# Projection stage of a hybrid attention block: x loaded four pieces ahead, reciprocal roots as logarithm and exponential, rotary key late, w_uq in four parts

## Chip, cores and metric

The kernel runs on the eight NeuronCores of one Trainium2 chip. The metric is device time in microseconds of the slowest core. Each core has TensorE (matmuls), VectorE, ScalarE, GpSimd and the SP queue engine; SP, ScalarE and GpSimd also issue DMAs. The cores do not exchange data or wait for one another inside the program.

## The reference

One layer over a sequence of 16 meta tokens and 4096 frames, batch 4, model width 4096. Only what the projection stage computes matters here:

```
u = rmsnorm(h) * norm_pre
z = u @ w_in        # diff q, k, v, gate; latent c_q (1536), c_kv (512); rotary key (64); mla gate
cq  = rmsnorm(cq) * g_cq;    q  = cq @ w_uq      # 16 heads x (128 + 64 rotary)
ckv = rmsnorm(ckv) * g_ckv;  kv = ckv @ w_ukv    # 16 heads x (128 key + 128 value)
k_rope = rope(kr);  q_rope = rope(q_rope)
```

Two attention groups follow (differential attention with ALiBi, and latent attention), each gated with silu; then one output projection with a norm and the residual. rmsnorm needs the reciprocal root of a mean of squares plus 1e-6.

## The kernel before, in words

Two cores share a batch element: each computes keys and values of all 4112 tokens and queries, gates and outputs of its own 2048 tokens. The work is in three stages: A, the projections (`stage_a`), B, the attention, and C, the output projection. The change touches A only.

The instruction order is written out by hand: `P.add` appends an operation to one engine's list, with tokens (`T`) for what it reads and writes; at the end waits on semaphores are derived from them. Each engine works through its own list in order, so an instruction that waits holds up all behind it on that engine. A DMA operation of several transfers (`dma=5`) has one wait ahead of the first and one semaphore for all. Background work is written as generators: `tick()` takes one step of `bg[0]`, and the matmul loops call it at fixed places, so that the background's instructions lie between those of the foreground.

Stage A goes through x in two phases, of four tiles with 512 tokens each, phase 0 also with a tile of 16 meta tokens (t = 4). The weights come in slabs of 256 columns (`load_upto`, on GpSimd's queue, f32 to bf16, three buffers, so slab i+3 waits for the last use of slab i).

- `prep(0, t)` loads a tile of x in 32 pieces of 128x512 f32 on ScalarE's queue into six buffers. For each piece ScalarE makes the scaled bf16 copy (L460), then the square (L466, L468), and VectorE adds the square to a sum (L469). Matmuls are L525 (columns of weights as the stationary operand) and L585 (tokens stationary). `stats` sums over partitions with a matmul (L474) and takes the reciprocal root (`rsqrt`, L426 to L428: VectorE, ScalarE, VectorE); `rtok_of` (L435) turns it to one value a token.
- The first three slabs are done tile by tile while x is read. The first tile's `prep` is written out before any matmul, that of the next tile lies in the ticks (42 a tile). `stats(0, t)` is written out whole after the first block of tile t; the steps of `prep_meta` (L492 to L496) lie in the first block of tile 3.
- Then `lam_of` computes the lambda of the differential attention from four loads, and slabs 3 to 18 of phase 0 run over the resident tiles while `prep(1, t)` reads the other half of x as background on SP's queue, with three buffers, writing it to DRAM (`UT`); phase 1 reads it back. Slab 3 is the rotary key (`job_kr`): after its matmuls VectorE multiplies with sine and cosine tables (L561 to L575), which SP loads behind the matmuls.
- Phase 1 repeats all key and value slabs and adds c_q, queries and gates. Results are evacuated through four bf16 buffers (`stb`) and stored by SP.
- Then the latent part: nine tiles of c_kv (512 tokens, the fifth has 16), each with 16 key blocks (`kn`, matmuls L792, evacuated by VectorE, L795) and 16 value blocks (`vm`, L803, ScalarE L806), 32 stores on SP; `norm_tile` for the next tile lies in the ticks (squares L729, sum L726, scaling L734). It is followed by four tiles of queries with `w_uq` (L825, L838). w_uq (four loads, one token) and the first two loads of c_q (1,536 KB each, SP) are issued ahead of the first c_kv tile.

What the program adds on each queue around the change:

```
for t in range(5):
    if t < 4:
        early[0] = stats(0, t)
        ...
    for i in range(3):
        run_slab(i, t)
```

Of the kernel before, what the change touches and what calls it, by code (L numbers as in the profile page):

```python
# [6 lines left out]
F32 = mybir.dt.float32  # L7
# [256 lines left out]
def build_nc():  # L264
# [50 lines left out]
    with stack:  # L315
# [23 lines left out]
        lams = A.alloc([8], F32)  # L339
        Tc = T("consts")  # L340
# [3 lines left out]
        ci = [0]  # L344

        def cload(dst, src):
            ci[0] += 1
            P.add('sp', lambda e: e.dma_start(out=dst, in_=src), writes=[Tc], dma=1, key=f'c{ci[0]}')

        cload(identf, ident_d)  # L350
        cload(gpre, gpre_d)
        cload(gcq, gcq_d)
        cload(gckv, gckv_d)
        cload(gsubB, gsub_d.partition_broadcast(128))
        P.add('dve', lambda e: e.tensor_copy(out=identb, in_=identf), reads=[Tc], writes=[Tc])
        P.add('dve', lambda e: e.memset(onesb, 1.0), writes=[Tc])
        P.add('dve', lambda e: e.memset(onesf, 1.0), writes=[Tc])
        P.add('dve', lambda e: e.tensor_scalar_mul(out=gsubB, in0=gsubB, scalar1=0.8), reads=[Tc], writes=[Tc])
# [4 lines left out]
            CK=CK, CQ=CQ, UT=UT, RP=RP, onesb=onesb, onesf=onesf, identf=identf, gpre=gpre, gcq=gcq, gckv=gckv, gsubB=gsubB, Tc=Tc,  # L363
# [13 lines left out]
def stage_a(nc, P, A, bank, Tb, DT, c):  # L377
# [3 lines left out]
    onesb, onesf, identf, gpre, gcq, gckv, gsubB, Tc = (c[k] for k in ['onesb', 'onesf', 'identf', 'gpre', 'gcq', 'gckv', 'gsubB', 'Tc'])  # L381
# [24 lines left out]
    def lam_of():  # L406
# [5 lines left out]
        for i in range(4):  # L412
            P.add('sp', lambda e, i=i: e.dma_start(out=lt4[:, i, :], in_=c['lam4_d'][i:i + 1, :].partition_broadcast(128)), writes=[Tlt], dma=1, key=f'lam{i}')
# [73 lines left out]

    def prep_meta():
        xa, Txa = fp.next()
        x3 = xa.rearrange("p (k t) -> p k t", k=32)  # L490
        P.add('sp', lambda e: e.dma_start(out=x3, in_=xTm), writes=[Txa], dma=1, key=('x', id(Txa)))
        P.add('dve', lambda e: e.tensor_tensor(out=uTm, in0=x3, in1=gpre.unsqueeze(2).to_broadcast([128, 32, 16]), op=ALU.mult), reads=[Txa, Tc], writes=[TuTm])  # L492
        P.add('act', lambda e: e.activation(out=xa, in_=xa, func=AF.Square), reads=[Txa], writes=[Txa])
        yield
        P.add('dve', lambda e: e.reduce_sum(out=Rpre[:, 2048:2064], in_=xa.rearrange("p (k t) -> p t k", k=32), axis=AX.X), reads=[Txa], writes=[TRp[4]])
        P.add('pe', lambda e: e.matmul(bank[SSB][:, 0:16], lhsT=onesf, rhs=Rpre[:, 2048:2064], start=True, stop=True), reads=[TRp[4], Tc], writes=[Tb[SSB]])  # L496
        rsqrt(Rpre[:, 2048:2064], bank[SSB][:, 0:16], 1.0 / D, [Tb[SSB]], TRp[4])
        yield
# [38 lines left out]
    def job_fm(dst_fn):  # L537
        def run(t, buf, Tw):
            ti = tile_of(t)
            wv = buf.rearrange("p (k n) -> p k n", k=32)  # L540
            for blk in range(2):
                b = mm_fm(ti, wv, Tw, 128 * blk)
                if early[0] is not None:
                    for _ in early[0]:
                        pass
                    early[0] = None
                dst, dTs = dst_fn(blk, ti)
                evac_scaled(b, ti, dst, dTs)
                tick()
        return run  # L550

    def job_kr(t, buf, Tw):
# [103 lines left out]
    for _ in gen:  # L656
        pass
# [761 lines left out]
```

How the kernel before makes its waits and increments, by code:

```python
                def body(eng, ops=ops):  # L143
                    waited = {}
                    for op in ops:
                        w = {}
                        for d in need[id(op)]:
                            k = d.sem.num
                            if k not in w or w[k][1] < d.val:
                                w[k] = (d.sem, d.val)
                        for k, (s, v) in w.items():
                            if waited.get(k, 0) < v:
                                eng.wait_ge(s, v)
                                waited[k] = v
                        if op.fn is None:
                            continue
                        ins = op.fn(eng)
                        if op.dma:
                            if not isinstance(ins, (list, tuple)):
                                ins = [ins]
                            assert len(ins) == op.dma, (op.name, len(ins), op.dma)
                            for i in ins:
                                i.then_inc(op.sem, 16)
                        elif op.sig:
                            assert ins is not None, op.name
                            ins.then_inc(op.sem, 1)
```

## Time and profile before

| | us |
|---|---|
| median of 3 runs | 8583.3 (7669.49 to 8768.4) |
| profiled execution, its own time | 7663.14 |
| its span, slowest core (5) | 7661.6 |
| spans of the eight cores | 7628.7 to 7661.6, granted clock 0.969 to 0.971 |
| TensorE busy | 7024.5 (92%) |
| ScalarE busy | 2313.8 (30%) |
| VectorE busy | 1646.0 (21%) |

The profile is of one execution on its slowest core. PE is TensorE's matmuls, PEld its weight loads, DVE is VectorE, ACT ScalarE, POOL GpSimd, SP the queue engine; ACTq, SPq and POOLq are the issuing sides. "Granted clock" is TensorE's clock as a share of full speed. L123 is a line of the kernel before. Matmuls are pipelined, and a few of their records are missing. A wait is put down to what came last.

### The profile page before, as it was taken

To read this page: it belongs to the slowest core of one execution; us is meant where nothing else is said; L and a number is where in the kernel's file an instruction comes from. 1 tells how busy PE (TensorE), PEld (TensorE's weight loads), DVE (VectorE), ACT (ScalarE), POOL (GpSimd) and SP (SyncE) were. 2 spreads that over 40 slices of the span, in tenths; PEclk is the share of its full clock that TensorE was granted. 3 is DMA by queue.
4 is the path that set the end of the run, shared out by engine and by line. 5 is a ranking of instruction groups with operands and counts; after the bars stand their busy time and mean duration, and the time that the engine had idled before them with its cause. 6 is when DMAs were issued, how large, how long until landed. Compare 5 with 4: busy or idle time off the path is not lost.

```text
span 7661.6 us, 142140 instructions; the slowest of 8 cores (7628.7 to 7661.6 us)
## 1 busy us (share of the span) xinstructions
PE 7024.5 (92%) x55192; PEld 5012.4 (65%) x55192; DVE 1646.0 (21%) x3213; ACT 2313.8 (30%) x4442; POOL 314.3 (4%) x570
## 2 busy tenths in 40 slices
PE   3579999999999999999997999999999999979877
PEld 1234588644688444588885344677778888868767
DVE  2324400011000101111001565233331111132233
ACT  3401111000011000011111324888887877311111
POOL 0000000000000000000000000000011010000000
PEclk9789999999999999999998999999999999989989
DMA  5346732533232222333336432122155565365564
GB/s 119 103 94 153 167 80 51 140 75 63 53 62 55 57 59 54 65 72 82 72 77 138 137 116 84 53 84 91 57 152 152 157 179 148 137 220 187 186 213 175
DMA packets 493084, 846.03 MB, mean 110 GB/s; under 512 B 115140, under 2 KB 354820, under 8 KB 472328
## 3 DMA queue, kind: packets, MB, share of 16 engines
q0 software_dynamic: 73952, 447.75, 24.5%
q1 hardware_dynamic: 380456, 319.96, 14.0%
q10 hardware_dynamic: 38016, 69.22, 3.1%
q8 instruction: 450, 7.37, 0.4%
q14 instruction: 210, 1.72, 0.1%
HBM read 790.93 MB, written 234.12 MB: 134 GB/s over the span
## 4 chain that ended last, share of the span: by engine, by line
PE 80%; DVE 6%; DMA 4%; ACT 4%; issue 3%; SPq 1%; another core or an unknown queue 1%; ACTq 1%; DVEq 0%
PE ps L585 24%; PE ps L525 22%; PE ps L1269 10%; PE ps L985 10%; PE ps L1020 9%; PE ps L825 2%; DMA arena<-xo 1%; PE ps L803 1%; ACT arena L460 1%; PE ps L838 1%; DVE arena L469 1%; ACT arena L468 1%; PE ps L792 1%; ACT arena L1009 1%; DVE arena L1093 1%
## 5 line engine op out<-in xcount | busy, mean ns | idle before, releaser
L525 PE MATMUL ps<-arena 128*128 128x512 bf16 (+1 forms) x9632 | 1997.8, 368 | 172.0 <-ACT arena L460 133.7
L585 PE MATMUL ps<-arena 128*128 128x256 bf16 (+1 forms) x16640 | 1819.3, 273 | 0.0
L585 PEld LDWEIGHTS ps<-arena 128*128 128x128 bf16 (+1 forms) x16640 | 1625.1, 98 | 194.0 <-issue 3.2
L525 PEld LDWEIGHTS ps<-arena 128*128 128x128 bf16 x9632 | 900.2, 98 | 1266.5 <-issue 233.6
L1020 PE MATMUL ps<-arena 128*128 128x129 bf16 (+3 forms) x9216 | 1194.8, 248 | 72.7 <-ACT arena L1009 43.5
L985 PE MATMUL ps<-arena 128*128 128x256 bf16 (+2 forms) x8576 | 1222.7, 261 | 3.2 <-issue 3.2
L1269 PE MATMUL ps<-arena 128*128 128x256 bf16 x8192 | 918.2, 276 | 136.6 <-DMA arena<-MIX 87.8
L1269 PEld LDWEIGHTS ps<-arena 128*128 128x128 bf16 x8192 | 811.0, 99 | 243.4 <-issue 139.7
L1020 PEld LDWEIGHTS ps<-arena 128*128 128x128 bf16 (+1 forms) x9216 | 749.6, 98 | 274.5 <-issue 198.6
L1009 ACT ACTIVATE arena<-ps,arena 128x512 bf16<-128x512 f32 (+3 forms) x1352 | 787.9, 622 | 111.1 <-PE ps L985 56.7
L985 PEld LDWEIGHTS ps<-arena 128*128 128x128 bf16 (+1 forms) x8576 | 713.3, 97 | 117.4 <-issue 45.4
L1006 ACT ACTIVATE arena<-ps 128x512 bf16<-128x512 f32 (+2 forms) x1216 | 687.5, 574 | 177.7 <-PE ps L985 83.0
L534 DVE TENSOR_TENSOR arena<-ps,arena 128x512 bf16<-128x512 f32 (+1 forms) x292 | 190.1, 654 | 2047.5 <-PE ps L525 2035.1
L590 ACT ACTIVATE arena<-ps,arena 128x256 bf16<-128x256 f32 (+1 forms) x264 | 124.8, 474 | 1352.3 <-PE ps L585 1334.4
L1275 ACT ACTIVATE arena<-arena 128x256 bf16<-128x256 f32 x256 | 106.6, 417 | 922.7 <-DVE arena L1272 672.8
L596 ACT ACTIVATE arena<-ps,arena 128x256 f32<-128x256 f32 x256 | 121.4, 474 | 763.2 <-PE ps L585 759.9
L639 POOL DMA_DIRECT2D arena<-w_in x264 | 140.4, 551 | 3391.9 <-PE ps L525 1724.5
L1272 DVE COPY arena<-ps 128x256 f32<-128x256 f32 x256 | 108.0, 424 | 729.9 <-PE ps L1269 715.6
L468 ACT ACTIVATE arena<-arena 128x512 f32<-128x512 f32 x248 | 156.1, 629 | 341.4 <-DVE arena L463 330.0
L469 DVE TENSOR_TENSOR arena<-arena 128x512 f32<-128x512 f32 x248 | 171.6, 692 | 359.7 <-ACT arena L468 359.5
L596 ACT ACT_TABLE_LOAD x2 | 2.6, 1283 | 777.5 <-PE ps L585 777.5
L803 PE MATMUL ps<-arena 128*128 128x512 bf16 (+1 forms) x528 | 138.0, 384 | 67.7 <-DVE arena L795 67.7
(98 smaller groups left out, 2535.0 us busy)
## 6 DMA issues: line engine op xcount, KB each, us to landing
arena<-w_in POOLq DMA_DIRECT2D x264, 512.0 KB, 12.8
arena<-WOB POOLq DMA_DIRECT2D x64, 2048.0 KB, 9.0
arena<-xT ACTq DMA_DIRECT2D x128, 256.0 KB, 2.8
arena<-xT SPq DMA_DIRECT2D x128, 256.0 KB, 3.6
arena<-w_out POOLq DMA_DIRECT2D x16, 2048.0 KB, 33.6
WOB<-arena POOLq DMA_DIRECT2D x16, 2048.0 KB, 10.7
arena<-xo ACTq DMA_DIRECT2D x128, 256.0 KB, 9.6
out<-arena SPq DMA_DIRECT2D x128, 256.0 KB, 5.4
```

Of the source, the lines that this page charges most:

```text
L468: P.add('act', lambda e, xa=xa: e.activation(out=xa, in_=xa, func=AF.Square), reads=[Txa], writes=[Txa])
L469: P.add('dve', lambda e, xa=xa: e.tensor_tensor(out=sm, in0=sm, in1=xa, op=ALU.add), reads=[Txa, Tsm], writes=[Tsm])
L525: P.add('pe', lambda e, k=k: e.matmul(bank[b][:, 0:n], lhsT=wv[:, k, col:col + 128], rhs=ti['u'](k), start=(k == 0), stop=(k == 31)), read ...
L534: P.add('dve', lambda e: e.tensor_tensor(out=sb[:, 0:n], in0=bank[b][:, 0:n], in1=ti['R'], op=ALU.mult), reads=[Tb[b], ti['TR']], writes=[ ...
L585: P.add('pe', lambda e, k=k, c0=c0, nt=nt, b=b: e.matmul(bank[b][0:nt, 0:256], lhsT=ti['u'](k)[:, c0:c0 + nt], rhs=wv[:, k, :], start=(k = ...
L803: P.add('pe', lambda e, k=k: e.matmul(bank[b][0:nt, :], lhsT=cn[:, k, c0:c0 + nt], rhs=wkv[:, k, 2048 + 512 * g:2048 + 512 * g + 512], sta ...
L825: P.add('pe', lambda e, b=b, h=h, k=k, cn=cn: e.matmul(bank[b], lhsT=wq[:, k, 128 * h:128 * h + 128], rhs=cn[:, k, :], start=(k == 0), sto ...
L985: P.add('pe', lambda e, lh=lh, rh=rh, a=a, b_=b_, m=m, i=i, n=len(steps): e.matmul(S[0:nk, 256 * m + a:256 * m + b_], lhsT=lh, rhs=rh, sta ...
L1006: P.add('act', lambda e, o_=o_, i_=i_: e.activation(out=o_, in_=i_, func=AF.Exp, scale=scale), reads=[Tb[sbk]], writes=[Tpt])
L1009: P.add('act', lambda e, o_=o_, i_=i_, ci_=ci_: e.activation(out=o_, in_=i_, func=AF.Exp, bias=abias[0:nk, ci_:ci_ + 1], scale=scale), rea ...
L1020: P.add('pe', lambda e, m=m, qb=qb, rhs=rhs, last=last: e.matmul(bank[OB[2 * qb + m]][:, 0:E + 1], lhsT=pt[0:nk, 256 * m + 128 * qb:256 * ...
L1269: P.add('pe', lambda e, k=k: e.matmul(bank[b][:, 0:256], lhsT=m[:, k, :], rhs=w[:, k, :], start=(k == 0), stop=(k == 31)), reads=[Tw, Tm[0 ...
```

## The change

Everything lies in stage A and in the constants ahead of it. (1) The five constants are loaded by one operation of five transfers, gpre first, where each was an operation that waited for the one before; lambda's four loads likewise. (2) `prep` of phase 0 keeps four loads ahead instead of five, in the same six buffers. (3) `rsqrt` is a logarithm and an exponential on ScalarE. (4) `stats` is taken in single steps, one after the first block of each slab; the meta tokens are loaded at the start and their matmul comes later. (5) The rotary key slab moves from position 3 to 15 in both phases, its tables are loaded one tile ahead, and background work is finished before it. (6) w_uq is loaded as four operations at different times, each with a token of its own, and the first two c_q loads move into the c_kv loop. (7) In `norm_tile` the scaling operations are spread over more ticks.

```diff
+        P.add('sp', lambda e: [e.dma_start(out=dst, in_=src) for dst, src in ((gpre, gpre_d), (identf, ident_d), (gcq, gcq_d), (gckv, gckv_d), (gsubB, gsub_d.partition_broadcast(128)))],
+              writes=[Tc], dma=5, key='c')
...
+        P.add('dve', lambda e: e.memset(epsc, EPS), writes=[Tc])
...
-        for i in range(4):
-            P.add('sp', lambda e, i=i: e.dma_start(out=lt4[:, i, :], in_=c['lam4_d'][i:i + 1, :].partition_broadcast(128)), writes=[Tlt], dma=1, key=f'lam{i}')
+        P.add('sp', lambda e: [e.dma_start(out=lt4[:, i, :], in_=c['lam4_d'][i:i + 1, :].partition_broadcast(128)) for i in range(4)], writes=[Tlt], dma=4, key='lam')
...
     def rsqrt(dst, src, inv, rT, wT):
-        P.add('dve', lambda e: e.tensor_scalar(out=dst, in0=src, scalar1=inv, scalar2=EPS, op0=ALU.mult, op1=ALU.add), reads=rT, writes=[wT])
-        P.add('act', lambda e: e.activation(out=dst, in_=dst, func=AF.Sqrt), reads=[wT], writes=[wT])
-        P.add('dve', lambda e: e.reciprocal(out=dst, in_=dst), reads=[wT], writes=[wT])
+        P.add('act', lambda e: e.activation(out=dst, in_=src, func=AF.Ln, bias=epsc[:, 0:1], scale=inv), reads=rT + [Tc], writes=[wT])
+        P.add('act', lambda e: e.activation(out=dst, in_=dst, func=AF.Exp, scale=-0.5), reads=[wT], writes=[wT])
...
@@ def stats
         P.add('pe', lambda e: e.matmul(bank[SSB], lhsT=onesf, rhs=row, start=True, stop=True), reads=[Trow, Tc], writes=[Tb[SSB]])
-        yield
         rsqrt(row, bank[SSB], 1.0 / D, [Tb[SSB]], Trow)
...
+    def load_meta():
+        P.add('sp', lambda e: e.dma_start(out=acc, in_=xTm), writes=[Tacc], dma=1, key='xm')
+
     def prep_meta():
-        xa, Txa = fp.next()
...
+        P.add('dve', lambda e: e.reduce_sum(out=Rpre[:, 2048:2064], in_=acc.rearrange("p (k t) -> p t k", k=32), axis=AX.X), reads=[Tacc], writes=[TRp[4]])
+        for _ in range(6):
+            yield
         P.add('pe', lambda e: e.matmul(bank[SSB][:, 0:16], lhsT=onesf, rhs=Rpre[:, 2048:2064], start=True, stop=True), reads=[TRp[4], Tc], writes=[Tb[SSB]])
         rsqrt(Rpre[:, 2048:2064], bank[SSB][:, 0:16], 1.0 / D, [Tb[SSB]], TRp[4])
-        yield
+        for _ in range(6):
+            yield
...
@@ def job_fm
-                if early[0] is not None:
-                    for _ in early[0]:
-                        pass
-                    early[0] = None
+                if early[0] is not None and blk == 0:
+                    next(early[0], None)
...
@@ def job_kr
-        ck, Tck = fp.next()
-        sk, Tsk = fp.next()
...
+        if not krt:
+            kr_tables(ti)
+        ck, Tck, sk, Tsk = krt.pop(0)
+        if t < (4 if phase_[0] == 0 else 3):
+            kr_tables(tile_of(t + 1))
...
-        out.insert(3, ('kr', 0, job_kr))
         for sl in range(8):
             out.append(('w', C_DV + 256 * sl, job_tm('v', sl)))
+        out.insert(15, ('kr', 0, job_kr))
...
     load_upto(1)
-    gen = prep(0, 0, xfp, 5, 'act')
-    for _ in gen:
+    load_meta()
+    for _ in prep(0, 0, xfp, 4, 'act'):
         pass
...
-            if t < 3:
-                bg[0] = prep(0, t + 1, xfp, 5, 'act')
-            else:
-                bg[0] = prep_meta()
+            bg[0] = prep(0, t + 1, xfp, 4, 'act') if t < 3 else prep_meta()
         for i in range(3):
             run_slab(i, t)
-        while bg[0] is not None:
-            tick()
+        for gen in (early, bg):
+            while gen[0] is not None:
+                if next(gen[0], 'end') == 'end':
+                    gen[0] = None
...
         load_upto(i + 3)
+        if every[i][0] == 'kr':
+            while bg[0] is not None:
+                tick()
+            fp.items = xfp
...
@@ def norm_tile
         rsqrt(acc[:, 0:n], bank[SSB][:, 0:n], inv, [Tb[SSB]], Tacc)
         yield
+        yield
...
-            if k % 2 == 1:
+            if KC_ == 4 or k % 2 == 1:
                 yield
...
+    def load_wq(rT):
+        j = len(Twq) // 3
+        lo = 16384 + 9216 * j
+        t = heir(*[x for a in range(lo // 16384, (lo + 9215) // 16384 + 1) for x in TuT[a]])
+        Twq.extend([t] * 3)
+        P.add('pool', lambda e: e.dma_start(out=wq[:, 3 * j:3 * j + 3, :], in_=w_uq[:, 9216 * j:9216 * j + 9216].rearrange("p (k n) -> p k n", k=3)), reads=rT, writes=[t], dma=1, key=('wq', j))
...
+        elif t == 1:
+            load_wq([])
...
-    q_load(0)
-    q_load(1)
...
-    Twq = heir(*(TuT[1] + TuT[2] + TuT[3]))
-    P.add('pool', lambda e: [e.dma_start(out=wq[:, 3 * k:3 * k + 3, :], in_=w_uq[:, 9216 * k:9216 * k + 9216].rearrange("p (k n) -> p k n", k=3)) for k in range(4)], writes=[Twq], dma=4, key='wq')
...
     for j, (g0, n) in enumerate(kvt):
...
+        if j in (0, 2, 5):
+            load_wq([Tcn])
+        if j in (1, 4):
+            q_load(j // 4)
```

## Rows read from the trace of the kernel before

**Rows 1.** Busy us by stretch: its length, engines, granted clock, DMA share, GB/s.

```profile
0.00:451.50 451.50, 215.60 (x1004) 91.73 (x1004) 121.24 (x174) 174.81 (x263) 8.22 (x19) 0.84 0.38 97
...
451.50:642.60 191.10, 144.43 (x685) 63.33 (x684) 72.38 (x129) 23.64 (x37) 7.48 (x15) 0.88 0.63 140
...
642.60:4119.90 3477.30, 3477.26 (x24675) 2384.05 (x24676) 361.67 (x612) 313.86 (x626) 128.10 (x241) 1.00 0.37 79
...
4119.90:4449.00 329.10, 246.67 (x1151) 107.64 (x1150) 148.92 (x206) 105.27 (x186) 2.12 (x4) 0.90 0.54 147
```

**Rows 2.** Waits of TensorE to 451.5 us: line, awaited, us in total, times, longest.

```profile
PE ps L525 <- ACT arena L460: 133.7, 54, 33.8
...
PE ps L435 <- DVE arena L428: 67.1, 4, 20.9
...
PE ps L496 <- DVE arena L495: 32.3, 1, 32.3
```

**Rows 3.** DMA issues of the first 35 us: transfer, count, size, median us to landing.

```profile
arena<-gpre SPq DMA_DIRECT2D x1, 16.0 KB, 11.9
...
arena<-w_in POOLq DMA_DIRECT2D x4, 512.0 KB, 15.0
```

**Rows 4.** Timeline of the pass over x: start us, us, instruction, idle time before it.

```profile
31.51 1.28 ACT L460 ACT_TABLE_LOAD   x1 [31.51 <-DVE arena L358]
...
54.08 0.72 ACT L460 ACTIVATE arena<-arena 128x512 bf16<-128x512 f32 x1 [1.36 <-DVE arena L469]
...
56.84 0.72 ACT L460 ACTIVATE arena<-arena 128x512 bf16<-128x512 f32 x1 [1.31 <-DVE arena L469]
...
116.58 0.71 ACT L460 ACTIVATE arena<-arena 128x512 bf16<-128x512 f32 x1
...
117.92 0.71 ACT L460 ACTIVATE arena<-arena 128x512 bf16<-128x512 f32 x1
...
118.95 3.58 ACTq L451 DMA_DIRECT2D arena<-xT  x6
...
122.63 0.72 ACT L460 ACTIVATE arena<-arena 128x512 bf16<-128x512 f32 x1 [3.29 <-DMA arena<-xT]
```

**Rows 5.** Timeline around the end of the first tile loop.

```profile
385.35 0.71 ACT L460 ACTIVATE arena<-arena 128x512 bf16<-128x512 f32 x1
...
410.34 41.19 PE L525 MATMUL ps<-arena 128*128 128x512 bf16 x352
...
454.00 32.02 SPq L413 DMA_DIRECT2D arena<-lam  x4
```

**Rows 6.** Waits of TensorE between 451 and 643 us.

```profile
PE ps L525 <- DVE arena L573: 22.7, 4, 8.5
...
PE ps L525 <- DMA arena<-w_kr: 7.6, 1, 7.6
```

**Rows 7.** Waits of TensorE between 4119.9 and 4449 us.

```profile
PE ps L803 <- DVE arena L795: 67.7, 11, 52.2
...
PE ps L792 <- DVE arena L795: 6.1, 2, 3.1
```

**Rows 8.** Timeline of the first latent tile.

```profile
4129.93 3.35 DVE L428 RECIPROCAL arena<-arena 128x512 f32<-128x512 f32 x1 [2.79 <-ACT arena L427]
...
4136.89 49.12 SPq L423 DMA_DIRECT2D KN<-arena  x1
```

**Rows 9.** DMA issues between 4119 and 4195 us.

```profile
arena<-CQ SPq DMA_DIRECT2D x2, 1536.0 KB, 67.8
```

**Rows 10.** DMA issues of x, between 70 and 130 us, then between 145 and 385.

```profile
arena<-xT ACTq DMA_DIRECT2D x22, 256.0 KB, 4.5
...
arena<-xT ACTq DMA_DIRECT2D x84, 256.0 KB, 2.8
```

**Rows 11.** The chain of waits: start us, us, what.

```profile
95.78 18.04 DMA arena<-xT
```

**Rows 12.** ScalarE's groups, whole span: count, busy us, mean ns, idle before.

```profile
L1009 ACT ACT_TABLE_LOAD x1 | 1.3, 1283 | 2.3 <-PE ps L985 2.3
```

More of the change, by code:

```diff
@@ L339, in build_nc @@
         lams = A.alloc([8], F32)
+        epsc = A.alloc([1], F32)
         Tc = T("consts")
@@ L342, in build_nc @@
         const_base = A.off
[L344 to L354, printed above, removed]
+        P.add('sp', lambda e: [e.dma_start(out=dst, in_=src) for dst, src in ((gpre, gpre_d), (identf, ident_d), (gcq, gcq_d), (gckv, gckv_d), (gsubB, gsub_d.partition_broadcast(128)))],
+              writes=[Tc], dma=5, key='c')
         P.add('dve', lambda e: e.tensor_copy(out=identb, in_=identf), reads=[Tc], writes=[Tc])
@@ L362, in build_nc @@
             xT=xT, xTm=xTm, w_in=w_in, w_kr=w_kr, w_uq=w_uq, w_ukv=w_ukv, KD=KD, VD=VD, GD=GD, QD=QD, QN=QN, QR=QR, KN=KN, KR=KR, VM=VM, GM=GM,
-            CK=CK, CQ=CQ, UT=UT, RP=RP, onesb=onesb, onesf=onesf, identf=identf, gpre=gpre, gcq=gcq, gckv=gckv, gsubB=gsubB, Tc=Tc,
+            CK=CK, CQ=CQ, UT=UT, RP=RP, epsc=epsc, onesb=onesb, onesf=onesf, identf=identf, gpre=gpre, gcq=gcq, gckv=gckv, gsubB=gsubB, Tc=Tc,
             lams=lams, Tlam=Tlam, lam4_d=lam4_d, cosk_d=cosk_d, sink_d=sink_d, cosq_d=cosq_d, sinq_d=sinq_d))
@@ L380, in stage_a @@
     CK, CQ, UT, RP = c['CK'], c['CQ'], c['UT'], c['RP']
-    onesb, onesf, identf, gpre, gcq, gckv, gsubB, Tc = (c[k] for k in ['onesb', 'onesf', 'identf', 'gpre', 'gcq', 'gckv', 'gsubB', 'Tc'])
+    epsc, onesb, onesf, identf, gpre, gcq, gckv, gsubB, Tc = (c[k] for k in ['epsc', 'onesb', 'onesf', 'identf', 'gpre', 'gcq', 'gckv', 'gsubB', 'Tc'])
     uo = A.off
@@ L486, in idle @@
             yield
+    def load_meta():
+        P.add('sp', lambda e: e.dma_start(out=acc, in_=xTm), writes=[Tacc], dma=1, key='xm')
     def prep_meta():
-        xa, Txa = fp.next()
[L490 to L493, printed above, removed]
-        yield
-        P.add('dve', lambda e: e.reduce_sum(out=Rpre[:, 2048:2064], in_=xa.rearrange("p (k t) -> p t k", k=32), axis=AX.X), reads=[Txa], writes=[TRp[4]])
+        x3 = acc.rearrange("p (k t) -> p k t", k=32)
+        P.add('dve', lambda e: e.tensor_tensor(out=uTm, in0=x3, in1=gpre.unsqueeze(2).to_broadcast([128, 32, 16]), op=ALU.mult), reads=[Tacc, Tc], writes=[TuTm])
+        P.add('act', lambda e: e.activation(out=acc, in_=acc, func=AF.Square), reads=[Tacc], writes=[Tacc])
+        P.add('dve', lambda e: e.reduce_sum(out=Rpre[:, 2048:2064], in_=acc.rearrange("p (k t) -> p t k", k=32), axis=AX.X), reads=[Tacc], writes=[TRp[4]])
+        for _ in range(6):
+            yield
         P.add('pe', lambda e: e.matmul(bank[SSB][:, 0:16], lhsT=onesf, rhs=Rpre[:, 2048:2064], start=True, stop=True), reads=[TRp[4], Tc], writes=[Tb[SSB]])
         rsqrt(Rpre[:, 2048:2064], bank[SSB][:, 0:16], 1.0 / D, [Tb[SSB]], TRp[4])
-        yield
+        for _ in range(6):
+            yield
         rtok_of(0, 4, 1, 16, Rpre[:, 2048:2064], TRp[4])
@@ L550, in job_fm, with kr_tables @@
         return run
+    krt = []
+    def kr_tables(ti):
+        n, g0 = ti['n'], ti['g0']
+        ck, Tck = fp.next()
+        sk, Tsk = fp.next()
+        P.add('sp', lambda e: e.dma_start(out=ck[:, 0:n], in_=c['cosk_d'][:, g0:g0 + n]), writes=[Tck], dma=1, key=('x', id(Tck)))
+        P.add('sp', lambda e: e.dma_start(out=sk[:, 0:n], in_=c['sink_d'][:, g0:g0 + n]), writes=[Tsk], dma=1, key=('x', id(Tsk)))
+        krt.append((ck, Tck, sk, Tsk))
     def job_kr(t, buf, Tw):
@@ L556, in job_kr @@
         b = mm_fm(ti, wv, Tw, 0)
-        ck, Tck = fp.next()
-        sk, Tsk = fp.next()
-        P.add('sp', lambda e: e.dma_start(out=ck[:, 0:n], in_=c['cosk_d'][:, g0:g0 + n]), writes=[Tck], dma=1, key=('x', id(Tck)))
-        P.add('sp', lambda e: e.dma_start(out=sk[:, 0:n], in_=c['sink_d'][:, g0:g0 + n]), writes=[Tsk], dma=1, key=('x', id(Tsk)))
+        if not krt:
[3 more added lines that the diff above has]
+            kr_tables(tile_of(t + 1))
         P.add('dve', lambda e: e.tensor_tensor(out=ck[:, 0:n], in0=ck[:, 0:n], in1=ti['R'], op=ALU.mult), reads=[Tck, ti['TR']], writes=[Tck])
@@ L752, in stage_a @@
     wkv, Twkv = uT[:, 0].rearrange("p k t -> p (k t)").rearrange("p (k n) -> p k n", k=4), heir()
+    uflat = uT.rearrange("p a k t -> p (a k t)")
+    wq = uflat[:, 16384:16384 + 36864].rearrange("p (k n) -> p k n", k=12)
+    Twq = []
+    def load_wq(rT):
[4 more added lines that the diff above has]
+        P.add('pool', lambda e: e.dma_start(out=wq[:, 3 * j:3 * j + 3, :], in_=w_uq[:, 9216 * j:9216 * j + 9216].rearrange("p (k n) -> p k n", k=3)), reads=rT, writes=[t], dma=1, key=('wq', j))
     for t in range(4):
@@ L844, in stage_a @@
     A.note(uo, 32768, Twkv)
-    A.note(uo + 32768, 73728, Twq)
+    A.note(uo + 32768, 73728, *Twq)
     for i in range(2):
```

6 lines of the change are left out of this document (2 added, 4 removed).

## The prediction

> **What bounds the kernel now.** I read the busy times of TensorE by stretch first. Of the 7661.6 us span, TensorE works without a gap between 642.6 and 4119.9 us, so nothing changed there can pay. Three stretches are different [rows 1]: the first 451.5 us (215.6 busy, 235.9 idle), 451.5 to 642.6 (46.7 idle) and 4119.9 to 4449.0 (82.4 idle, at a mean clock of 0.90). All lie in the projection stage, and every edit acts on one of them.
>
> Then the waits of TensorE in each. In the first it waits 133.7 us for the copy of x on ScalarE, 67.1 us before the L435 matmuls for a reciprocal, and once 32.3 us for the statistics of the meta tokens [rows 2]. So ScalarE's pass over x sets the pace. The start-up rows show why that pass begins late: gpre alone takes 11.9 us because x and weights are already moving, each constant waits for the one before, and ScalarE's first work is the table load at 31.51 [rows 3, 4]. The timeline shows the rhythm: a copy starts each 2.76 us (54.08, 56.84), and ahead of it ScalarE is idle for 1.36 us until VectorE's sum L469 frees the buffer for the next load; at a tile's end, where no load is issued, copies start 1.33 us apart [rows 4].
>
> In the second stretch VectorE is late: the four loads for lambda occupy SP's queue from 454.00 for 32.02 us [rows 5], and the rotary key's products (L573) then cost TensorE 22.7 us; first it waits 7.6 us for w_kr [rows 6]. In the third, 67.7 us of waits for the cast L795 hold one of 52.2 [rows 7], when SP's issue of a KN store stands for 49.12 us behind two CQ loads, which land in 67.8 us while w_uq's four parts are in flight [rows 8, 9].
>
> **The pass over x.** Four ahead instead of five, in six buffers: the load issued at piece k reuses the buffer of k-2, whose sum ended during piece k-1. The wait goes; what is late next is ScalarE itself. Its cycle is the bare 1.33 plus one issue; the issue row is 0.33 (118.95, 3.58 for six, so up to 0.60 with its gap), and I take 0.44: 1.77 us [rows 4]. A tile is 28x1.77 + 3x1.33 = 53.5 us from first to last copy; tile to tile 4.7 (117.92 to 122.63, rows 4); three root pairs in the path at about 1.5 (two operations near 0.63, as the old root); last copy 0.7. Sum 4x53.5 + 3x4.7 + 4.5 + 0.7 = 233 us. The same recipe for before (27x2.76 + 4x1.33 a tile, the roots as one operation) gives 336, and the trace has 385.4 + 0.7 - 32.8 = 353 [rows 4, 5], so 17 us are waits for x itself. As the weight slabs 1 and 2 now collide with faster loads (an x load lands in 4.5 us there instead of 2.8, rows 10), I take 20. Bounds: nothing extra, or a mean cycle of 2.1 us (+37).
>
> **The start.** The five constants go out at once, gpre first, and nothing waits between them. The last can't land later than the 11.9 us of gpre behind x, give or take its issue: about 13 to 15, then VectorE's constants (1.4) and the table load (1.28). First copy at 17 instead of 32.8 (31.51 + 1.28, rows 4); between 13 and 24. TensorE needs the first slab, which lands about 15 us after its issue, near 19 [rows 3]: it catches up during the pass. Pass ends at 17 + 233 + 20 = 270 instead of 386.
>
> **The tail of the first tile loop.** Meta's matmul leaves the middle of block 0, and the statistics' small matmuls no longer stand in front of block 1. After the pass TensorE has the f32 sum (2), five blocks and meta (41.2 as the row of 352 matmuls, rows 5), and the small matmuls at the end (2): 46 us, where before it took 65.5. It ends at 316 instead of 451.5: **-135.5**.
>
> **Slab 3.** Its buffer is freed only by slab 0's last tile. It now is a full slab, four loads like those of rows 3, instead of w_kr, which has half the columns (7.6 us of wait, rows 6). By the first slab's 15 us from issue [rows 3] the wait is about 13: **+5.5** (0 to 9).
>
> **Rotary key late, lambda at once.** The 22.7 us behind L573 go; of the 46.7 idle only the slab wait and perhaps 2 us stay, since VectorE's backlog came from the 32.02 us on SP's queue and the key. Matmuls in this stretch ran at a mean clock of 0.88; a stretch without gaps ran at 1.00, worth about 10 us of the 144.4 busy [rows 1]. Gain 37 + 10: **-47** (-30 to -57). Where the key goes (sixteenth slab), TensorE has no idle time, its background work is spent (four tiles of 41 steps against 140 ticks of the seven key slabs left and nine for each value slab), and its tables are issued a tile early. VectorE's six products and sum for a tile take under 6 us against 6.9 us of matmuls, with seven banks of cover: 0. Without that cover the price is the 4 to 8 us a tile seen before.
>
> **The roots.** L428 is 3.35 us of VectorE [rows 8], L426 near 0.7 by the like-sized sums. They go; ScalarE gets one operation more. Thirteen of the 22 lie in the latent stage, in front of casts that free banks. The waits other than the 52.2 sum to 15.5 (L795 for L803) and 6.1 (L792) [rows 7]; with the scaling split into single yields they go: **-21** (0 to -21).
>
> **w_uq in four parts, CQ loads later.** The 52.2 goes: a CQ load of 1,536 KB [rows 9] has SP's queue to itself at the second and the fifth tile, and the parts run in the silu slabs and in tiles 1, 3 and 6. With the slow matmuls behind the stop, -54. Four parts took near 68 us together with CQ, so about 14 to 17 each; they now share with 32 stores a tile. Twelve store buffers and seven banks cover about 16 us. I take 11 us of new stops (0 to 40). GpSimd's queue holds nothing else in those tiles; each later part waits for a norm that was done a tile earlier. The rows by themselves can't say whether w_uq or the CQ loads blocked SP [rows 8, 9].
>
> The Trainium skill (DMA: Bandwidth & Descriptors, "Queues, rings and completion order") says that an engine takes turns between queue rows packet by packet; then w_uq can at most halve the stores' rate, the blame is the CQ loads', and the new stops are near 0. No row here separates the two; the sum keeps its 11.
>
> **Sum.** -135.5 + 5.5 - 47 - 21 - 54 + 11 = -241 us. Against the profiled execution's 7663.1 us (span 7661.6): **7422**, said as 7420. TensorE is full right behind each stretch, and the cores don't wait for each other, so I expect nothing given back. The median of the runs shown, 8583, holds two that lie 12 to 14% above that execution; the forecast is for executions like the profiled one (lowest 7669).
>
> **Rivals.**
> (1) x can't follow. For: loads took 18 us once in the slab collision [rows 11]. Against: the median is 2.8 us [rows 10], and four pieces ahead give 7.1. A mean cycle of 2.3 costs 128x0.53 = 68: 7490. Chance 0.10.
> (2) Stops in the latent stage stay: three parts of w_uq each stop the stores, 14 us a part, and each CQ load 5 to 10. 11 becomes about 60, and the 21 of the roots are hidden by them: 7490. Chance 0.10.
> (3) Logarithm and exponential lie in different table sets, so each root pays two loads of 1.28 (the one ahead of the exponentials of stage B, as an example) [rows 12]. The logarithms of stage B (L1100) run between exponentials with that single load, which speaks against. Three in the pass, thirteen in the latent stage where part is covered: 8 + 15 = 23: 7445. Chance 0.04, inside the forecast's range. The Trainium skill (ScalarE: Activation LUTs, "What ACT_TABLE_LOAD costs") adds a drain of 1.38 us to each switch; by it 23 would be about 48.
> (4) Slower: the eight cores' faster reading of x starves the first pass. To cancel the 241 us the mean cycle has to rise from 1.77 by 1.88 to 3.65, that is, landings over 14.6 us for all 128 pieces; at 18 us (the collision's worst) a cycle is 4.5, +350 us, and the kernel takes 7770. Only single loads came near. Chance 0.03.
> (5) The change does less than it says, the pace stays set by the sum: -241 + 107 (108 cycles of 0.99 more) = 7530. Chance 0.05: the buffer arithmetic speaks against it.
>
> Forecast 0.68. A change of 2% (153 us) is what a measurement of this kernel can tell from none: below 7510 is faster. Range 7365 (no new stops, start at 13, full clock) to 7530 (cycle 2.1 with part of 2, or 5). Faster 0.88 (forecast and rivals 1 to 3, less 0.04 for two of them together), same 0.08 (5 and those), slower 0.04 (4, and a hundredth for what isn't seen).
>
> **What would show it.** Copies of x 1.7 to 1.9 us apart and no wait for L469; first copy near 17; the pass's last copy near 270; full TensorE from about 330 on; no wait over 10 us in the latent stage; no more table loads than now. Wrong would be: waits of ScalarE for x in every tile, a stop behind KN stores while a part of w_uq flies, a table load at every root.

## The result

| | before | changed |
|---|---|---|
| executions comparable with one another, us | 7669 | 7377 to 7398 |
| ratio | | 0.962 (95% interval 0.958 to 0.966) |
| profiled execution, span of its slowest core | 7661.6 | 7385.8 |
| median span of the eight cores in it | 7651.4 | 7363.3 |

The forecast was 7420, range 7365 to 7530, faster. The median of the changed kernel's four executions is 7392.5, that of the three in the table 7387.4. In some executions of either kernel the cores of a die run at a lower clock and the time is up to 14% longer; the ratio is taken without them, and of a profile with such cores the other die is read. The saving between the profiled executions is 276 us where the sum had 241. The forecast is against the profiled execution's 7663 us: against the 8583 us median shown before, the same 7420 would announce 13.5% less, and the kernels differ by 3.8%.

The changed kernel by stretch, cut at the same places of the program as [rows 1] (end of the first tile loop, first latent matmul, first query matmul). Columns: stretch, its length, busy time and count of TensorE, its weight loads, VectorE, ScalarE and GpSimd, granted clock, DMA share, GB/s:

```profile
0.00:287.90 287.90, 201.92 (x1004) 87.81 (x1004) 104.97 (x165) 172.38 (x268) 9.36 (x22) 0.96 0.60 152
287.90:3910.90 3623.00, 3607.98 (x25356) 2444.66 (x25356) 414.92 (x730) 337.74 (x666) 135.51 (x255) 1.00 0.37 84
3910.90:4182.70 271.80, 246.23 (x1150) 108.37 (x1149) 117.18 (x188) 109.98 (x195) 1.06 (x2) 0.97 0.55 162
```

The first loop fell from 451.5 to 287.9 us (-163.6; forecast -135.5), the stretch to the latent part from 3668.4 to 3623.0 (-45.4; forecast +5.5 - 47), the latent part from 329.0 to 271.8 (-57.2; forecast -21 - 54 + 11 = -64). The rest took 9.6 us less; no code there changed, and that stretch varies by as much between cores and kernels. TensorE is busy for nearly as long as before (6990 us against 7024): mostly idle time went. The 34 us of busy time that went too are the same number of matmuls in less time: 13.7 of them lie in the first loop, where the mean granted clock rose from 0.84 to 0.96, and 13.7 in the stretch to the latent part, whose first 191 us ran at 0.88 before [rows 1].

TensorE's waits of the changed kernel to 650 us (line, what it awaited, total us, times, longest), and those of the latent part:

```profile
PE ps L518 <- ACT arena L451: 79.9, 40, 27.8
PE ps L518 <- DMA arena<-w_in: 15.0, 1, 15.0
PE ps L465 <- DVE arena L460: 4.3, 4, 1.2
```

```profile
PE ps L820 <- DVE arena L812: 13.9, 4, 8.0
PE ps L731 <- ACT arena L734: 8.7, 21, 1.0
```

The rows of each run name the lines of that run's own kernel. In the changed kernel L451 is the copy of x, L459 its square, L460 the sum, L518 a matmul with weights stationary, L465 the small matmul of the statistics. L809 and L820 are the latent key and value blocks, L812 and L823 their evacuations, L731 and L734 a norm's matmul and squares. In the experiments' kernels the same operations stand a few lines off.

Against [rows 2] the small matmuls' 67.1 us and meta's 32.3 are gone, and the wait for the copy of x is 79.9 instead of 133.7. Against [rows 6] the rotation's 22.7 are gone and the slab wait is 15.0 instead of 7.6. Against [rows 7] 13.9 stand for 67.7.

The pass over x in the changed kernel's timeline (start us, us, instruction, idle before it); these answer to [rows 4]:

```profile
23.95 0.23 DVE L347 CAST arena<-arena 128x128 bf16<-128x128 f32 x1 [23.95 <-DMA arena<-gsub]
...
26.80 0.72 ACT L451 ACTIVATE arena<-arena 128x512 bf16<-128x512 f32 x1
...
110.47 0.72 ACT L451 ACTIVATE arena<-arena 128x512 bf16<-128x512 f32 x1
...
111.28 0.63 ACT L459 ACTIVATE arena<-arena 128x512 f32<-128x512 f32 x1
111.36 0.33 ACTq L442 DMA_DIRECT2D arena<-xT  x1
111.82 0.71 ACT L451 ACTIVATE arena<-arena 128x512 bf16<-128x512 f32 x1
```

Copies start 1.35 us apart (110.47, 111.82), over five of them 1.39 (the median of the pass is 1.40), and no row shows ScalarE waiting for VectorE's sum. The issue at 111.36 lies inside the square that runs from 111.28 to 111.91: ScalarE's queue issues the load while its engine works. The last copy starts at 238.3 instead of 385.4. The first starts at 26.80, because VectorE's constants wait for gsub until 23.95. The DMA issues of the first 35 us (transfer, size, median us to landing) against [rows 3]:

```profile
arena<-gsub SPq DMA_DIRECT2D x1, 128.0 KB, 20.9
...
arena<-gpre SPq DMA_DIRECT2D x1, 16.0 KB, 2.7
```

### The profile page after: what moved, and what is told of

It reads as the page before. It is cut to its first block, busy times and chain, and to the rows that moved or that the text cites. A ratio compares the mean times of both kernels' runs of the same rounds, so it can differ in the third digit from the quotient of the medians.

```text
span 7385.8 us, 141959 instructions; the slowest of 8 cores (7351.6 to 7385.8 us)
## 1 busy us (share of the span) xinstructions
PE 6990.1 (95%) x55192; PEld 5001.5 (68%) x55192; DVE 1568.0 (21%) x3170; ACT 2316.3 (31%) x4461; POOL 314.8 (4%) x570
## 4 chain that ended last, share of the span: by engine, by line
PE 84%; DVE 5%; DMA 3%; issue 3%; ACT 3%; SPq 2%; ACTq 1%; DVEq 0%; POOL 0%; POOLq 0%
PE ps L518 25%; PE ps L587 25%; PE ps L1286 10%; PE ps L1002 10%; PE ps L1037 9%; PE ps L842 1%; PE ps L820 1%; DMA arena<-xo 1%; ACT arena L451 1%; SPq L1233 1%; PE ps L809 1%; DVE arena L1110 1%; DVE arena L1111 1%; PE ps L855 1%; DVE arena L1112 1%
## 5 line engine op out<-in xcount | busy, mean ns | idle before, releaser
L518 PE MATMUL ps<-arena 128*128 128x512 bf16 (+1 forms) x9632 | 1975.8, 366 | 94.9 <-ACT arena L451 79.9
L518 PEld LDWEIGHTS ps<-arena 128*128 128x128 bf16 x9632 | 897.0, 98 | 1173.8 <-issue 129.5
L459 ACT ACTIVATE arena<-arena 128x512 f32<-128x512 f32 x248 | 156.1, 629 | 270.4 <-DVE arena L454 258.8
L460 DVE TENSOR_TENSOR arena<-arena 128x512 f32<-128x512 f32 x248 | 171.7, 692 | 262.1 <-ACT arena L459 261.9
L842 PE MATMUL ps<-arena 128*128 128x512 bf16 x768 | 175.3, 383 | 8.7 <-DVE arena L575 6.4
```

Source lines behind the costliest of these rows:

```text
L459: P.add('act', lambda e, xa=xa: e.activation(out=xa, in_=xa, func=AF.Square), reads=[Txa], writes=[Txa])
L460: P.add('dve', lambda e, xa=xa: e.tensor_tensor(out=sm, in0=sm, in1=xa, op=ALU.add), reads=[Txa, Tsm], writes=[Tsm])
L518: P.add('pe', lambda e, k=k: e.matmul(bank[b][:, 0:n], lhsT=wv[:, k, col:col + 128], rhs=ti['u'](k), start=(k == 0), stop=(k == 31)), read ...
L842: P.add('pe', lambda e, b=b, h=h, k=k, cn=cn: e.matmul(bank[b], lhsT=wq[:, k, 128 * h:128 * h + 128], rhs=cn[:, k, :], start=(k == 0), sto ...
```

## The experiments

The table gives medians over the eight cores of a profiled execution (cores 4 to 7 for the old root, 0 to 3 for lambda), each core cut at the same places of the program: first copy of x, last minus first copy, end of the first tile loop, wait for the fourth slab, from the loop's end to the first latent matmul, the latent part. It leaves out the last part of the kernel, which no edit touches and which swings by 10 to 20 us. The whole execution's time is given with each experiment.

| kernel | first copy | pass | loop end | slab wait | to latent | latent |
|---|---|---|---|---|---|---|
| before | 31.1 | 352.0 | 449.6 | 7.3 | 3668.2 | 326.4 |
| changed | 25.0 | 210.5 | 285.0 | 13.8 | 3621.4 | 268.7 |
| changed, once more | 25.5 | 210.1 | 284.9 | 13.1 | 3622.5 | 268.4 |
| loads four ahead alone | 31.4 | 230.6 | 328.6 | 7.6 | 3668.2 | 326.9 |
| old root | 25.8 | 223.4 | 300.1 | 14.1 | 3626.3 | 280.8 |
| w_uq in one go | 25.2 | 210.6 | 285.0 | 12.9 | 3621.2 | 301.4 |
| c_q early | 26.4 | 210.5 | 286.2 | 13.3 | 3620.9 | 268.2 |
| key early | 25.4 | 210.8 | 285.6 | 6.8 | 3655.6 | 268.2 |
| lambda serial | 25.3 | 210.2 | 284.4 | 13.0 | 3621.2 | 268.0 |
| x issued by SP | 24.3 | 213.7 | 286.8 | 12.4 | 3620.8 | 270.4 |
| gpre's own token | 5.7 | 224.1 | 279.8 | 12.9 | 3621.4 | 268.4 |
| statistics whole | 25.1 | 213.3 | 294.2 | 13.7 | 3621.4 | 269.4 |

**Loads four ahead, alone, in the kernel before.**

```diff
-    gen = prep(0, 0, xfp, 5, 'act')
+    gen = prep(0, 0, xfp, 4, 'act')
...
-                bg[0] = prep(0, t + 1, xfp, 5, 'act')
+                bg[0] = prep(0, t + 1, xfp, 4, 'act')
```

> The kernel before with one edit: x loaded four pieces ahead instead of five in phase 0. Theory (the sum's buffer was the whole wait, and ScalarE issues a load while its last operation still runs): copies of x 1.40 us apart instead of 2.76, the first still at 32.8 us, last copy near 260 instead of 385, first tile loop ends near 335 instead of 451.5, the rest of the trace unchanged; span about 7545. Rival A (the issue adds to the cycle, as in the forecast): copies 1.77 us apart, last copy near 295, span about 7570. Rival B (the early loads alone give little, the small matmuls behind the old root hold TensorE and through it the pass): last copy after 330, span over 7600.

The time was 7540 us, the first loop ended 121 us earlier, and nothing after it moved. One number changed in two calls is 44% of the whole gain. The last copy starts at 262, as the theory had it, not near 295. ScalarE's waits there (awaited, total us, times):

```profile
ACT arena L460 <- DMA arena<-xT: 25.9, 13, 3.9
...
ACT arena L460 <- DVE arena L469: 14.5, 3, 4.9
```

In the profile before ScalarE idled 143.2 us over 94 waits for L469; 3 are left, and they stand where the reciprocal or TensorE's pace holds VectorE.

**The old root in the changed kernel.** `rsqrt` is again multiply-add, square root and reciprocal.

> The changed kernel with the old reciprocal root (multiply-add on VectorE, square root on ScalarE, reciprocal of 3.35 us on VectorE), all else as changed. Theory (the reciprocal in VectorE's list holds the casts that free banks in the latent stage): latent stage 15 to 25 us longer than 271.8, waits of its value matmuls for the cast back; first tile loop at most 5 us longer, since the small matmuls stay deferred; span 7400 to 7415. Rival (the spread of the scaling did it, the root costs nothing): latent stage within 5 us of 271.8, span 7385 to 7395.

The execution took 7500.5 us, set by cores 0 to 3. Cores 4 to 7 span 7393 to 7422 us, those of the changed kernel 7352 to 7386. The latent part is 12.1 us longer, with waits like these on core 4, where the changed kernel has 13.9 and 2.0:

```profile
PE ps L821 <- DVE arena L813: 18.7, 7, 6.5
...
PE ps L810 <- DVE arena L813: 5.5, 5, 3.1
```

That is under the 15 to 25 expected. The first loop is 15.1 us longer, where at most 5 were expected: with a pass this quick the root does stand in it. ScalarE waits for sums held up behind the reciprocal and for VectorE's part of the root (core 4 again, to 260 us):

```profile
ACT arena L452 <- DVE arena L461: 8.2, 3, 2.8
ACT arena L419 <- DVE arena L418: 6.3, 4, 1.8
```

So the root is worth about 27 us plus 5 in the middle, not the 21 forecast, and half of it lies in the first loop.

**w_uq in one go**, ahead of the latent tiles, c_q loads still late.

```diff
-        elif t == 1:
-            load_wq([])
...
+    P.add('pool', lambda e: [e.dma_start(out=wq[:, 3 * k:3 * k + 3, :], ...) for k in range(4)], writes=[Twq[0]], dma=4, key='wq')
     for j, (g0, n) in enumerate(kvt):
...
-        if j in (0, 2, 5):
-            load_wq([Tcn])
```

> The changed kernel with w_uq loaded in one go ahead of the first latent tile, as before, while the two c_q loads stay in tiles 1 and 4. Theory Q (the c_q loads ahead of the stores in SP's own queue made the 52 us stop): no stop over 15 us, latent stage 272 to 285 us. Theory W (w_uq takes the DMA engines from the stores): a stop of 30 us or more in the first two or three tiles, latent stage 300 us or more.

7416 us; the latent part is 32.7 us longer. No c_q load is in flight (the first is issued at 3989), and SP stands still all the same. Theory W's latent time came (301.4), but as three stops of TensorE and not as one of 30 us. The timeline of its slowest core, and TensorE's stops (19.7, 12.1 and 12.1 us):

```profile
3925.78 28.43 SPq L415 DMA_DIRECT2D VM<-arena  x1
3954.31 13.11 SPq L415 DMA_DIRECT2D KN<-arena  x1
```

```profile
3948.64 1.87 PE L818 MATMUL ps<-arena 128*128 128x512 bf16 x4 [19.66 <-DVE arena L810]
...
3962.58 1.86 PE L807 MATMUL ps<-arena 128*128 128x512 bf16 x4 [12.08 <-ACT arena L821]
...
3976.56 1.86 PE L818 MATMUL ps<-arena 128*128 128x512 bf16 x4 [12.12 <-DVE arena L810]
```

**c_q early**, w_uq still in four parts.

```diff
+    q_load(0)
+    q_load(1)
     for j, (g0, n) in enumerate(kvt):
...
-        if j in (1, 4):
-            q_load(j // 4)
```

> The changed kernel with the two c_q loads issued ahead of the first latent tile, as before, while w_uq stays in four parts. Theory Q (c_q in SP's queue): a stop of 15 to 30 us in the first tile, since 3 MB stand ahead of the stores and share with one part of w_uq, latent stage 285 to 300 us. Theory W (w_uq takes the engines): no stop over 10 us, latent stage within 8 us of 271.8.

7381 us, the latent part as in the changed kernel. The c_q loads by themselves stop nothing; theory Q fell in both runs. The run is narrower than its theory says, though: the part of w_uq ahead of these loads, issued at 3881.72, had landed by 3901 (17 to 18.5 us a part), and the loads went out at 3910.73, so they never met one. They landed in 12.8 us, where in the kernel before, beside w_uq in one go, they took 67.8:

```profile
arena<-CQ SPq DMA_DIRECT2D x2, 1536.0 KB, 12.8
```

How w_uq does it shows in the DMA queues (kind, packets, MB, share of the 16 engines). First 3924 to 3964 us of the run with w_uq in one go, then 4130 to 4180 of the kernel before:

```profile
q0 software_dynamic: 399, 6.47, 95.5%
q1 hardware_dynamic: 399, 0.36, 3.7%
```

```profile
q0 software_dynamic: 488, 8.11, 95.8%
q1 hardware_dynamic: 489, 0.50, 4.2%
```

q0 is GpSimd's queue with w_uq, q1 SP's, in the first run with the stores. Both got the same number of packets, 399 and 399, 488 and 489. But a packet of w_uq carries 16 KB on average (6.47 MB / 399) and one of the stores 0.9 KB, so the stores moved 0.36 MB in 40 us, 9 GB/s, where a tile wants to store 4 MB in 28 us.

In the kernel before, what stood in q1 was above all the two c_q loads, with one KN store behind them [rows 8]:

```profile
4121.44 15.04 SPq L720 DMA_DIRECT2D arena<-CQ  x2
```

The 0.50 MB in 50 us are mostly theirs; from 4180 to 4190 us, with w_uq through, q1 moved 2.29 MB. So there w_uq held the c_q loads, and they stood ahead of the store. What their place cost beside w_uq in one go was not run. The latent part fell by 57.7 us (medians); w_uq's parts (32.7) and the root (12.1) leave 12.9 for the place of c_q, the spread of the scaling in `norm_tile`, which was not run alone either, and what these do only together. The Trainium skill (DMA: Bandwidth & Descriptors, "Queues, rings and completion order") says that the engines change queues packet by packet; the counts agree to one packet. The forecast drew the wrong conclusion from it: equal turns are not equal bytes.

Four parts help because each lands in 17 to 20 us, when the store buffers have only just run out, and two of them are issued ahead of the latent tiles (3855.60 and 3884.04). The two parts that start inside a tile (GpSimd's issues) are each followed by a short stop of TensorE, 4.43 and 7.99 us in the changed kernel:

```profile
3954.71 0.53 POOL L768 DMA_DIRECT2D arena<-w_uq  x1 [70.14 <-DVE arena L740]
4047.89 0.53 POOL L768 DMA_DIRECT2D arena<-w_uq  x1 [92.65 <-DVE arena L812]
```

```profile
3973.76 1.86 PE L820 MATMUL ps<-arena 128*128 128x512 bf16 x4 [4.43 <-DVE arena L812]
...
4068.84 1.86 PE L820 MATMUL ps<-arena 128*128 128x512 bf16 x4 [7.99 <-DVE arena L812]
```

**The rotary key early** in the changed kernel.

```diff
-        if t < (4 if phase_[0] == 0 else 3):
-            kr_tables(tile_of(t + 1))
...
+        out.insert(3, ('kr', 0, job_kr))
         for sl in range(8):
             out.append(('w', C_DV + 256 * sl, job_tm('v', sl)))
-        out.insert(15, ('kr', 0, job_kr))
...
-        if every[i][0] == 'kr':
-            while bg[0] is not None:
-                tick()
-            fp.items = xfp
```

> The changed kernel with the rotary key slab back at position 3 and its tables loaded behind its matmuls, in both phases; lambda's loads stay at once. Between the end of the first tile loop and the first latent matmul the changed kernel takes 3618 to 3623 us, the one before 3665 to 3679. Theory K (the key's products in VectorE's list, late behind table loads, made the waits): the wait for the slab falls from 15 to about 8, waits behind the rotation of 4 to 8 us for each tile come back, this stretch 3635 to 3650. Theory L (lambda's serial loads made VectorE late, the key was only standing in the queue): no wait behind the rotation, stretch 3611 to 3618.

7415 us. The stretch is 34.2 us longer, although the slab wait is 7.0 shorter: the key's place is worth 41 us, together with its tables' early load, which this edit takes back too. The stretch, 3655.6, is above theory K's 3635 to 3650. The waits from the loop's end to 640 us of its slowest core that the changed kernel doesn't have:

```profile
PE ps L518 <- DVE arena L573: 12.9, 3, 4.6
PE ps L465 <- DVE arena L460: 9.4, 1, 9.4
PE ps L518 <- DVE arena L527: 8.1, 3, 4.0
```

**Lambda's loads in series** in the changed kernel: `for i in range(4)` with one operation each.

> The changed kernel with lambda's four loads one after the other, as before; the rotary key stays late. Same stretch (3618 to 3623 us as changed). Theory K: VectorE is late by some 35 us, seven banks at 6.9 us cover it, stretch within 6 us of the changed kernel's. Theory L: waits of TensorE for the evacuation, stretch 3635 us or more.

The execution took 7600.9 us, set by cores 4 to 7. Cores 0 to 3 span 7358 to 7378 us, those of the changed kernel 7354 to 7374, and no stretch moved by more than 0.7. On core 3 SP is held for 35 us and VectorE idle for 38.65, and TensorE waits for nothing but the slab:

```profile
289.81 34.99 SPq L406 DMA_DIRECT2D arena<-lam  x4
...
327.96 0.29 DVE L409 TENSOR_TENSOR arena<-arena 128x128 f32<-128x128 f32 x1 [38.65 <-DMA arena<-lam]
```

By itself, with the key late, this edit is worth 0. That the seven banks cover VectorE's delay is the reading; the trace shows only that TensorE doesn't wait. With the key early too, which is the kernel before, the stretch is 12.6 us longer than with the key early alone (3668.2 against 3655.6). A part of that can be the old root; the two were not separated there.

**x issued by SP** instead of ScalarE (`prep(0, ..., 4, 'sp')`).

> The changed kernel with x of phase 0 loaded from SP's queue instead of ScalarE's. Theory (ScalarE issues a load beside its running operation, so the issue costs it 0.07 us of 1.40 a piece): copies 1.33 us apart where x is there, pass 5 to 10 us shorter than 209 to 212, first tile loop at most 5 us shorter, since TensorE's own 46 us a tile are nearly the pace. Rival (the issue costs its full 0.34 us somewhere on ScalarE): pass 25 us shorter or more. Rival 2 (loads behind stores in SP's list come late): pass longer than 215.

7401 us, pass 213.7 instead of 210.5, loop end 286.8 instead of 285.0. On the slowest core the copies start 1.33 us apart (median) instead of 1.40, so the issue on ScalarE costs the 0.07 us that the theory had, far from its full 0.33. But the pass isn't 5 to 10 us shorter: the waits for x are 39.0 us against 30.9, and the first pieces of tiles 2 and 3 are waited for 6.1 and 6.2 us where the changed kernel waits 2.9 and 3.2. Rival 2 is nearer, though its 215 wasn't reached.

**gpre with a token of its own**: the other constants are loaded apart, and what reads them is written behind the first tile's pass.

```diff
-        P.add('sp', lambda e: [e.dma_start(out=dst, in_=src) for dst, src in ((gpre, gpre_d), ...)], ...
...
+        P.add('sp', lambda e: e.dma_start(out=gpre, in_=gpre_d), writes=[Tg], dma=1, key='g')
...
-    ... activation(out=uT[:, t, k, :], ..., scale=gpre[:, k:k + 1]), reads=[Txa, Tc], ...
+    ... activation(out=uT[:, t, k, :], ..., scale=gpre[:, k:k + 1]), reads=[Txa, c['Tg']], ...
```

> The changed kernel with a token of its own for gpre; the other constants are read only after the first tile's pass, and VectorE's operations on them are written behind it. Theory (the copies wait for gsub, a broadcast that lands 21 us after its issue, while gpre lands after 2.7): first copy at 6 to 9 us instead of 23 to 27, x and the first slab now share the DMA engines, TensorE starts near 19, first tile loop ends 8 to 15 us earlier, at 268 to 278. Rival (the first slab and x set the start anyway): loop end within 4 us of 282 to 288.

7383 us. The first copy starts at 5.7 instead of 25.0, and the loop ends only 5.2 us earlier, at 279.8: that is the rival's range and not the 8 to 15 us of the theory. The pass is 13.6 us longer. TensorE now waits 27.0 us for the first slab, so it starts at 27.0 where it started at 27.8 in the changed kernel (the other of the two waits below, 14.9, is the one for the fourth slab), and in the first 80 us the DMA engines move x and three slabs at 186 GB/s and are busy for 89% of the time, against 82% in the changed kernel:

```profile
PE ps L522 <- ACT arena L455: 48.0, 34, 5.9
PE ps L522 <- DMA arena<-w_in: 41.9, 2, 27.0
```

**Statistics whole**: `stats` and meta's steps placed as before, meta's load still early.

> The changed kernel with the statistics written out whole after a tile's first block and meta's matmul back in the middle of tile 3's first block, as before; meta's load stays early and the new root stays. Theory (the deferral is worth what is left of the first loop's gain after the loads, the start and the root): pass within 8 us of 209 to 212, first tile loop ends 15 to 25 us later than 282 to 288, with waits of TensorE before the small matmuls. Rival (with the short root nothing waits there): loop end within 6 us.

7389 us, loop end 9.2 us later, between theory and rival, with 19.9 us of waits before the small matmuls on core 1 (longest 10.8) that the changed kernel doesn't have.

**Two versions meant to beat both.** The first has gpre's own token, the loads of x running on over a tile's end, and meta's blocks behind tile 3's of the same slab:

```diff
+            elif phase == 0 and t < 3:
+                load(k + lead - 32, mt + 2)
...
         for i in range(3):
             run_slab(i, t)
+            if t == 3:
+                run_slab(i, 4)
```

> The changed kernel with gpre's own token, meta's blocks right behind tile 3's of the same slab (so the first slab's buffer is free two slabs earlier) and the loads of x running on over a tile's end. Theory: the wait for the fourth slab (15 us) goes, first tile loop ends near 275, span 20 to 27 us under the changed kernel's. Rival (the slabs that follow are late instead): the wait moves to the fifth slab, span within 8 us of the changed kernel's.

It took 7356.7 us (twice) beside 7379.6 to 7381.8 for the changed kernel on the same chip; ratio to the kernel before 0.961 (0.957 to 0.965). The slowest core spans 7355.2 against 7380.2, and the median core about 7343 against 7374. The wait for the fourth slab is gone and did not move on: TensorE has no wait between 250 and 640 us. The pair differs by less than the interval; what shows the gain is the missing wait, and the first latent matmul, which starts at 3876.0 instead of 3908.5 (medians of the cores). It is the quickest of the kernels run. The three edits in it weren't separated.

The second does the first loop with six banks side by side, piece by piece (`for k in range(32): for j in range(6): matmul(bank[bs[j]], ...)`), and loads three slabs at the start.

> The changed kernel with gpre's own token, loads of x running on over a tile's end, and in the first tile loop the six blocks of three slabs accumulated side by side in six banks, piece by piece, so that TensorE works on all three slabs while x arrives (six matmuls a piece take 1.3 us against 1.4 for the copy and square); the first three slabs are loaded at once. Theory: the 46 us of TensorE behind the last piece shrink to about 10, first tile loop ends at 240 to 255, the wait for the fourth slab stays at 15, span 28 to 42 us under the changed kernel's. Rival (three slabs at the start starve x, and the six banks must be emptied before the next tile): loop end 275 or later, no gain.

7375 to 7381 us, ratio 0.964 (0.961 to 0.967): no gain in the whole time, the rival was nearly right. The loop ends at 272 (median), and the first latent matmul starts at 3894.8 instead of 3908.5; on the slowest core the later parts take that back. It falls short of the theory's 28 to 42 us: on its slowest core TensorE's first steady run starts at 59.5, when the third slab has landed, and then it is TensorE itself, 44 us of matmuls a tile with the emptying of banks between, that takes the time:

```profile
PE ps L681 <- DMA arena<-w_in: 57.5, 3, 26.1
...
PE ps L681 <- DVE arena L535: 9.0, 6, 4.3
```

**The changed kernel again**, beside these.

> The changed kernel itself, beside the others on the same chip. Both theories: 7375 to 7400 us, ratio to the kernel before 0.960 to 0.966.

7379.6 to 7381.8 us, with median stretches within 1.1 us of the first profile's: the table's differences are good to about that.

## Why the prediction was right or wrong

**The pass over x.** Right in the mechanism, wrong in a size. The step that failed is the cycle: "the bare 1.33 plus one issue" was taken as 1.77 us, and it is 1.39, since the issue lies beside the running square. The row it came from (118.95, six issues) has ScalarE with nothing to do, so it shows how long issues take, not what they cost. For the 112 pieces with an issue that term was about 42 us too large. The pass took 212 us instead of 253: -141 for the forecast's -100. Its other terms held: tile to tile 4.3 to 4.6 us for 4.7, and of the 30.9 us of waits for x 9.0 stand at the tiles' first pieces, which the forecast counted there, so that 21.9 stand against its 20.

**The start.** Wrong: 26.8 instead of 17. The bound used was gpre's 11.9 us, a transfer of 16 KB; the last of the five is gsub's broadcast of 128 KB, and it landed 20.9 us after its issue, while x and the first slab were moving. The forecast priced the group by one small member. It hardly matters, as gpre's own token shows: 19 us at the front are 5 at the loop's end, since TensorE can't start before the first slab, which lets it begin at 27.0 us instead of 27.8, and the pass gets 13.6 us longer. That the DMA engines, busy for 89% of the first 80 us, stretch the pass was read from the trace and not tried.

**The tail.** 48.9 us from the last copy to the loop's end instead of the forecast's 46. Right. What the edits of the first loop are worth one by one: loads 121 (put into the kernel before), start 6 (the shift of the first copy), root 15 and deferral 9 (taken out of the changed kernel), together 151 of 164.6. The other 13 are open: meta's early load wasn't run alone, and some of it may come only with several edits together.

**Slab 3.** Forecast +5.5, measured +7.4 (15.0 against 7.6). Right, and avoidable.

**Rotary key and lambda.** Forecast -47 before the slab's +5.5; the stretch lost 45.4 with a slab wait 7.4 longer, so -52.8. The split was wrong where it put lambda beside the key: lambda alone is 0 with the key late, the key with its tables 41. Of the 52.8 us, 13.7 are shorter matmuls, for the forecast's 10.

**Roots.** Forecast -21 in the latent part; 12 there, 15 in the first loop and 5 between. The forecast let the deferral of the small matmuls carry all of the first loop's part.

**w_uq and c_q.** The stop of 52 us went and small ones of 4.4 and 8.0 came, 12 together for the forecast's 11. The reason given beside the sum was wrong: splitting w_uq is worth 32.7 us, and moving c_q is worth nothing once w_uq is split.

**Rivals.** (1) and (4) fell: no x load was waited for longer than 5.1 us, and over the whole pass the copies start 1.67 us apart on average, waits included. (2) fell, its stops are 12 us and not 60. (3) fell: the whole projection stage has five table loads where the kernel before has seven, since the logarithm and the exponential share one:

```profile
L598 ACT ACT_TABLE_LOAD x2 | 2.6, 1283 | 776.7 <-PE ps L587 776.7
L418 ACT ACT_TABLE_LOAD x2 | 2.6, 1283 | 0.0
L451 ACT ACT_TABLE_LOAD x1 | 1.3, 1283 | 25.5 <-DVE arena L351 25.5
```

Nor is there a pause beside such a load: the one at 3869.98 us takes 1.28, ScalarE's operation before it ends at 3869.97, and the logarithm behind it starts at 3871.27. (5) fell with the cycle.

The errors partly cancel: the pass gave 41 us more than forecast, the start 10 less, the rest of the projection stage 6 less, and 10 us of the difference lie in the untouched last part. So the total is 35 us off, less than the one term that was 41 us too small; that much is luck.

## What to carry to other kernels

When an engine issues the loads into its own rotating buffers, an issue that waits for a buffer's last reader holds up that engine's work too, so load one piece less ahead than the buffers allow: with six buffers, five ahead put 94 waits of 143 us in all into the pass, four ahead left 3. When a bulk load and small stores share the DMA engines, compare their packets, not their bytes: at equal turns the stores got 0.36 MB of 6.83, so split the bulk load into pieces that are over by the time the store buffers run out. Before costing an issue on a compute engine's queue, look whether it lies inside a running operation of that engine.

## What was not expected of the hardware

GpSimd's converting load and SP's transfers took packets in strict turns, 399 to 399 and 488 to 489, with 16 KB and about 1 KB a packet. ScalarE's queue issued a DMA (0.33 us) while its engine ran the square, at a cost of 0.07 us in its rhythm: 1.40 us for two operations of 0.72 and 0.63, and 1.33 with the loads issued by SP. A 128 KB broadcast issued at 2.92 us landed 21 us later among 256 KB loads that landed in 3.2 (median) and weights in 16.
